# Seven products for eight transposed HGRN blocks, and token-major HGRN blocks in wide pairs

## Chip, cores, metric

One core of a Trainium2 chip runs the kernel. The metric is the device time of the run in microseconds (us); lower is better. The kernel before took 2633.77 us in the median of three runs (2633.15 to 2634.07).

## What is computed

One layer of an encoder on 1024 tokens of width 1024, in float32. Only the start of it matters here:

```python
z = rmsnorm(x, norm_mix_g[l])
proj = z @ w_in[l]                                   # 1024 x 1024 times 1024 x 11280
(ml_qk, ml_v, ml_o, ml_g, hg_q, hg_ff, hg_fb, hg_i, hg_g,
 gate_m, gate_h) = split_cols(proj, IN_SPLITS)
...
q_h = to_heads(jax.nn.silu(hg_q), HG_HEADS)          # per head a chunked scan, both directions,
v_h = to_heads(hg_i, HG_HEADS)                       # with forget gates from hg_ff and hg_fb
...                                                  # mLSTM, merge, W_out, cross attention,
x = x + (gelu(dwconv(up_a)) * up_b) @ w_down[l]      # and a gated FFN at the end
```

`hg_q`, `hg_ff` and `hg_fb` (3072 columns) are wanted transposed, channels by tokens. `hg_i` and `hg_g` (2048 columns) are wanted token-major.

## The kernel before, in words

Every engine has its own instruction stream, and they meet on semaphores. TensorE multiplies float32 in three passes of the fp32r type: each operand is split into a high part (a copy, `whi`, `a_hi`) and a low part (the rest, `wlo`, `a_lo`), and high x high, high x low and low x high are added up in PSUM.

Weights come in blocks (`Blk`). A block is 1024 rows x 256 columns, 1 MB, and goes to one of two slots of `raw`, by the parity of its number. For each block SP issues the load (`weights`, `stream`, L460) once the low part of the block two before is made; ACT makes the high part (`split_hi`, L853, a copy of 128x2048); DVE makes the low part (`split_lo`, L1383); PE multiplies; ACT copies the results out of PSUM to `ev` (`unit_out`, L864, four units of 512 columns a block) and issues their stores (`put_t`, `put_n`).

The stages around the change, in order:

- Nine blocks before it (memory keys and values, the mLSTM gates), till 85 us.
- `B_HGT`, 12 transposed blocks: `half_T` (L1979, matmul L1989) holds 128 weight columns stationary and moves 512 tokens. A block is 2 column tiles x 2 token halves x 8 contraction tiles x 3 passes = 96 matmuls of 512 columns. The first four blocks are written out, with the work on the mLSTM gate rows between them (DVE L1434 to L1463, ACT L955 to L960, PE's transposes of the gate rows at L2089 ahead of block 3); the other eight stand in a loop (L2092, ACT L971, DVE L1464). Results go to `hg_T` in DRAM.
- `B_HGN`, 8 token-major blocks: `half_N` (L2009, matmul L2020) holds 128 tokens stationary and moves the block's 256 weight columns, 8 token tiles x 8 x 3 = 192 matmuls of 256 columns. Results go to `hg_N`.
- `hg_pe` (L2099), 8 heads of the HGRN scan. Between its own small matmuls PE fills in the products of the mLSTM blocks (`dense`) in a fixed order. ACT's copy `level_keys` (L1016, L1026) and DVE's products feed it.

POOL meanwhile prepares the FFN's down projection, which is done much later: for each of 11 row blocks of `w_down` it loads 1 MB to `wd`, makes four sums of quarters (`quarter_sums`, L606, L611) in `wd_sums` and stores them, 1 MB, each step waiting for the one before (L616 to L621). Then it issues the loads of the first head's queries and gates (`load_q`, `qfb`, L629) when `hg_T` is complete, and of its values (`load_v`, L634) when `hg_N` is. The places of `wd` and `wd_sums` in SBUF are those of scan buffers.

The FFN's up projection (`win_pe`, L2414, matmul L2432) already uses the scheme of seven products: a block's product with all tokens is cut into 2 x 2 quarters (contraction halves, column or token halves), and seven products of sums of quarters replace eight. For a block of weights POOL makes four differences (`weight_sums`, L809, L817), ACT seven high parts (`factor_hi`, L1281) and one copy out of PSUM (L1328), DVE seven low parts (`factor_lo`, L1830) and seven additions out of PSUM (`product_out`, L1841). The sums of the input (four, of 128x2048) are made once (`operand_sum`, L1817, L1820; high parts L1268, low parts L1825). PE does 7 products x 4 contraction tiles x 3 passes = 84 matmuls of 512 columns. The down projection (`down_pe`, L2450) is made of seven products too, with tokens stationary and 512 columns moving.

## Time and profile before

| | |
|---|---|
| median of 3 runs | 2633.77 us |
| the profiled execution: its own time, its span | 2634.17 us, 2632.6 us |
| granted TensorE clock, mean | 0.995 |
| busy: PE matmul, DVE, ACT, POOL | 2591.4, 1462.5, 905.6, 607.0 us |
| busy share: DVE, ACT, POOL | 56%, 34%, 23% |
| DMA over the span | 348.96 MB, 133 GB/s |

The span runs from the first to the last instruction. PE is TensorE's matmuls, PEld its loads of the stationary side, which overlap them; DVE is VectorE, ACT ScalarE, POOL GpSimd, SP the engine that only issues DMAs. A matmul's duration includes its way through the array, so consecutive ones overlap: what one costs is the distance between starts. In a row, `out<-in xcount` tells the tiles written and read and the number of instructions; `L2020` is a line of the kernel.

### The profile page before, as it was taken

To read this page: it belongs to the slowest core of one execution; us is meant where nothing else is said; L and a number is where in the kernel's file an instruction comes from. 1 tells how busy PE (TensorE), PEld (TensorE's weight loads), DVE (VectorE), ACT (ScalarE), POOL (GpSimd) and SP (SyncE) were. 2 spreads that over 40 slices of the span, in tenths; PEclk is the share of its full clock that TensorE was granted. 3 is DMA by queue.
4 is the path that set the end of the run, shared out by engine and by line. 5 is a ranking of instruction groups with operands and counts; after the bars stand their busy time and mean duration, and the time that the engine had idled before them with its cause. 6 is when DMAs were issued, how large, how long until landed. Compare 5 with 4: busy or idle time off the path is not lost. (4 is left out here: it accounts for less than half of the span.)

```text
span 2632.6 us, 37140 instructions
## 1 busy us (share of the span) xinstructions
PE 2591.4 (98%) x14848; PEld 2277.7 (87%) x14848; DVE 1462.5 (56%) x1689; ACT 905.6 (34%) x1077; POOL 607.0 (23%) x553
## 2 busy tenths in 40 slices
PE   7999999999999999999999999999999999999998
PEld 7888899999999999988888788987798888888886
DVE  5511111277888888644443524343437998887566
ACT  6321211233343444322232523143314433343433
POOL 2014420011121222323331101000002565563001
PEclk9999999999999999999999999999999999999999
DMA  8345552223323333333431736101213232335754
GB/s 278 122 140 213 215 187 96 96 96 105 103 97 112 112 112 104 123 130 124 166 137 54 274 120 229 52 32 48 105 49 129 79 128 96 112 113 174 281 192 168
DMA packets 191426, 348.96 MB, mean 133 GB/s; under 512 B 9579, under 2 KB 125623, under 8 KB 191312
## 3 DMA queue, kind: packets, MB, share of 16 engines
q1 hardware_dynamic: 125152, 154.44, 17.7%
q0 software_dynamic: 32192, 118.44, 12.9%
q10 hardware_dynamic: 33968, 74.52, 7.4%
q8 instruction: 76, 1.25, 0.2%
q14 instruction: 38, 0.31, 0.0%
HBM read 241.10 MB, written 106.27 MB: 132 GB/s over the span
## 5 line engine op out<-in xcount | busy, mean ns | idle before, releaser
L2020 PE MATMUL ps<-whi,a_hi 128*128 128x256 f32 x1536 | 440.5, 287 | 0.8 <-DVE a_lo L1728 0.8
L2020 PE MATMUL ps<-whi,a_lo 128*128 128x256 f32 x1536 | 435.0, 283 | 0.0
L2020 PE MATMUL ps<-wlo,a_hi 128*128 128x256 f32 x1536 | 435.0, 283 | 0.0
L1386 DVE TENSOR_TENSOR wlo<-raw,whi 128x2048 fp32r<-128x2048 f32 x77 | 178.1, 2313 | 427.7 <-ACT whi L862 427.6
L1989 PE MATMUL ps<-a_hi,whi 128*128 128x512 f32 x864 | 347.7, 402 | 0.2 <-DVE a_lo L1405 0.2
L1989 PE MATMUL ps<-a_hi,wlo 128*128 128x512 f32 x864 | 336.9, 390 | 0.0
L1989 PE MATMUL ps<-a_lo,whi 128*128 128x512 f32 x864 | 336.5, 390 | 0.0
L867 ACT ACTIVATE ev<-ps 128x512 f32<-128x512 f32 x208 | 124.5, 598 | 508.2 <-PE ps L1989 290.2
L2020 PEld LDWEIGHTS ps<-whi,a_hi 128*128 128x128 f32 x1536 | 295.2, 192 | 1.6 <-DVE a_lo L1728 1.0
L2020 PEld LDWEIGHTS ps<-wlo,a_hi 128*128 128x128 f32 x1536 | 295.3, 192 | 0.4 <-issue 0.2
L2020 PEld LDWEIGHTS ps<-whi,a_lo 128*128 128x128 f32 x1536 | 295.0, 192 | 0.0
L862 ACT ACTIVATE whi<-raw 128x2048 fp32r<-128x2048 f32 x77 | 147.5, 1916 | 142.9 <-PE ps L2020 111.2
L1989 PEld LDWEIGHTS ps<-a_hi,wlo 128*128 128x128 f32 x864 | 162.2, 188 | 34.9
L1989 PEld LDWEIGHTS ps<-a_hi,whi 128*128 128x128 f32 x864 | 162.5, 188 | 31.7 <-DVE a_lo L1405 0.6
L1989 PEld LDWEIGHTS ps<-a_lo,whi 128*128 128x128 f32 x864 | 162.6, 188 | 31.2
L2130 PEld LDWEIGHTS ps<-X,Yc 128*128 128x128 f32 x896 | 114.6, 192 | 6.8 <-issue 2.4
L2130 PE MATMUL ps<-X,Yc 128*128 128x128 f32 x896 | 117.8, 285 | 0.2 <-DVE X L1547 0.2
L667 POOL TENSOR_TENSOR cv<-cv,cs 128x1024 f32<-128x1024 f32 x16 | 38.4, 2403 | 332.4 <-ACT cs L1034 332.4
L817 POOL TENSOR_TENSOR wt<-raw 128x512 f32<-128x512 f32 x36 | 82.6, 2296 | 136.3 <-DVE wlo L1830 97.5
L2432 PE MATMUL ps<-a_hi,whi 128*128 128x512 f32 x288 | 112.0, 389 | 0.0
L2432 PE MATMUL ps<-a_lo,whi 128*128 128x512 f32 x288 | 112.0, 389 | 0.0
L2432 PE MATMUL ps<-a_hi,wlo 128*128 128x512 f32 x288 | 112.0, 389 | 0.0
(360 smaller groups left out, 5403.9 us busy)
## 6 DMA issues: line engine op xcount, KB each, us to landing
raw<-in_w_in SPq DMA_DIRECT2D x45, 1024.0 KB, 5.0
raw<-in_w_up SPq DMA_DIRECT2D x22, 1024.0 KB, 5.1
hg_T<-ev ACTq DMA_DIRECT2D x24, 512.0 KB, 2.7
qfb<-hg_T POOLq DMA_DIRECT2D x24, 512.0 KB, 4.9
wd<-in_w_down POOLq DMA_DIRECT2D x11, 1024.0 KB, 5.3
down_weight_sums<-wd_sums POOLq DMA_DIRECT2D x11, 1024.0 KB, 4.7
hidden_T<-ga ACTq DMA_DIRECT2D x11, 1024.0 KB, 4.1
hidden_sums<-s POOLq DMA_DIRECT2D x10, 1024.0 KB, 4.9
```

The lines of the kernel that those rows point to most:

```text
L667: line(pool.tensor_tensor(cv[:], cv[:], cs[:], ALU.mult))
L817: signal(pool, pool.tensor_tensor(wt[:, i], x_, y_, ALU.subtract), s_t, weight_sum(n, i + 1))
L862: signal(act, act.activation(whi[:, b.slot], w4[:, b.slot], ACT.Copy), w_hi, b.count())
L867: signal(act, act.activation(ev[:, u], ps[:, u], ACT.Copy), ev_done, b.unit(u))
L1386: signal(dve, dve.tensor_tensor(wlo[:, b.slot], w4[:, b.slot], whi[:, b.slot], ALU.subtract), w_lo, b.count())
L1989: ins = pe.matmul(ps[:, u], W[sw][:, b.slot, k, c * P:(c + 1) * P], op[mw][:, k, t * HALF:(t + 1) * HALF], start=k == 0 and q == 0, stop=k ...
L2020: ins = pe.matmul(ps[:, u, part * BC:(part + 1) * BC], op[sw][:, k, t * P:(t + 1) * P], W[mw][:, b.slot, k], start=k == 0 and q == 0, stop ...
L2130: ins = pe.matmul(pair((l + 1) % 2, c), chunk(Yc, c), view(X, c * P, *dims), start=True, stop=True)
L2432: ins = pe.matmul(ps[:, bank], ring(W[sw], q)[:, k], op[mw][:, k], start=k == 0 and p_ == 0, stop=k == 3 and p_ == 2)
```

## The change

- The first four transposed blocks stay. The other eight (`B_HS`) are done with seven products of 84 matmuls in all, written out block by block. POOL makes the weights' four differences (`hs_weight_sums`), ACT and DVE the high and low parts quarter by quarter (`hs_hi`, `hs_lo`), ACT copies product 0 out and DVE adds the others out of PSUM (`hs_out`). Each of the seven products has its place in the weight buffer (`ring`).
- Four sums of the input are made between the first four blocks: two on DVE behind the first block's gate work, two after PE's gate transposes have read the gate rows, whose memory they share. DVE makes their low parts, ACT their high parts.
- The 8 token-major blocks become 4 pairs: a block is half the contraction (4 tiles) of 512 columns. PE goes through the 8 token tiles with the first block, one PSUM bank each, and again with the second, 768 matmuls of 512 columns in all. ACT copies out 8 banks per pair.
- The down-weight sums go behind `load_q(0)`. The next load of `wd` is issued once the sums have read it, just ahead of the store of the sums; each round waits for the load and for the last store. `wd` and `wd_sums` are moved to other scan buffers' places, and the first `level_keys` of ACT, the first convolution of DVE and POOL's `load_v(0)` wait for the last store.
- Semaphores of the FFN stages are shared with the new stage, with offsets on their counts.

```diff
+    sb("ahead_of_wd", [P, 14 * T - 2 * NT], F32, c)
     wd = sb("wd", [P, 2, D], F32, c)
+    sb("ahead_of_sums", [P, 2 * T], F32, c)
     wd_sums = sb("wd_sums", [P, 4, HALF], F32, c)
+with ExitStack() as c:
...
-    stream(B_HGN, 8, HG_N_COL)
+    with sp.Fori(0, 4) as i:
+        c = sp.snap(i * (2 * BC) + HG_N_COL)
+        for j in range(2):
+            b = Blk(B_HGN + j, i, 2)
+            sp.wait_ge(w_lo, b.count(-2))
+            sp.dma_start(wide(raw, b), w_in[:, 4 * j:4 * j + 4, at(c, 2 * BC)]).then_inc(w_ld[b.slot], 16)
...
-    for g in range(NFF):
-        pool.dma_start(wd[:], A["w_down"][0][g * BC:(g + 1) * BC, :].rearrange("(k p) n -> p k n", p=P)).then_inc(sum_io, 16)
-        pool.wait_ge(sum_io, 32 * g + 16)
+    def hs_weight_sums(n):
+        b = Blk(B_HS + n)
+        pool.wait_ge(w_ld[b.slot], b.slot_dmas())
+        if n:
+            pool.wait_ge(w_lo, b.count(-1))
+        b11, b12, b21, b22 = [w_quarter(b, k, c) for k in range(2) for c in range(2)]
+        for i, (x_, y_) in enumerate(((b12, b11), (b22, hwt[:, 0]), (b22, b12), (b21, hwt[:, 1]))):
+            signal(pool, pool.tensor_tensor(hwt[:, i], x_, y_, ALU.subtract), s_t, 4 * n + i + 1)
+    for n in range(N_HS):
+        hs_weight_sums(n)
+    def down_weights(g):
+        rows_ = A["w_down"][0][g * BC:(g + 1) * BC, :].rearrange("(k p) n -> p k n", p=P)
+        pool.dma_start(wd[:], rows_).then_inc(x_ld[3], 16)
+    def down_weight_sums(g):
+        pool.wait_ge(x_ld[3], 16 * g + 16)
+        if g:
+            pool.wait_ge(sum_io, 16 * g)
         line(quarter_sums(wd[:, 0, 0:HALF], wd[:, 0, HALF:D], wd[:, 1, 0:HALF], wd[:, 1, HALF:D], wd_sums, False))
+        if g + 1 < NFF:
+            down_weights(g + 1)
         pool.dma_start(wsum_d[g].rearrange("i p n -> p i n"), wd_sums[:]).then_inc(sum_io, 16)
-        pool.wait_ge(sum_io, 32 * g + 32)
...
+    down_weights(0)
+    for g in range(NFF):
+        down_weight_sums(g)
+    pool.wait_ge(sum_io, 16 * NFF)
     pool.wait_ge(st[0], 16 * 21)
     pool.wait_ge(st[1], 16 * 20)
...
+        if b.step or b.base != B_HS - 1:
+            split_hi(b.ahead(1))
+        else:
+            hs_sum_hi(2)
+            for q in range(3):
+                hs_hi(0, q)
...
+    def pair_out(b, col, t, stored):
+        u, c = t % 4, t // 2 % 2
+        if t % 2 == 0:
+            act.wait_ge(st[c], stored[c])
+        act.wait_ge(unit_done, b.unit(t))
+        signal(act, act.activation(ev[:, u], ps[:, t], ACT.Copy), ev_done, b.unit(t))
+        if t % 2:
+            act.dma_start(hN[(t - 1) * P:(t + 1) * P, at(col, 2 * BC)].rearrange("(u p) n -> p u n", p=P),
+                          ev[:, u - 1:u + 1]).then_inc(st[c], 16)
+    def pair_act(i, step, stored):
+        b = Blk(B_HGN, i, step) if step else Blk(B_HGN + 2 * i)
+        col = act.snap(i * (2 * BC)) if step else i * 2 * BC
+        split_hi(b.ahead(1))
+        split_hi(b.ahead(2), unit_done, b.unit(0))
+        for t in range(NT):
+            pair_out(b, col, t, [v + 16 * (t // 4) for v in stored])
...
+    def hs_sum_hi(i):
+        act.wait_ge(s_sum, i + 1)
+        signal(act, act.activation(hs[i][1][:], hs[i][0][:], ACT.Copy), hi_gelu, i + 1)
+    def hs_hi(n, q):
+        b = Blk(B_HS + n)
+        if q == 0:
+            act.wait_ge(w_ld[b.slot], b.slot_dmas())
+        if n:
+            act.wait_ge(prod_done if q < PRODUCTS - 1 else unit_done, hs_product(n - 1, q))
+        else:
+            act.wait_ge(unit_done, Blk(B_HS - (2 if q < 3 else 1)).unit(3))
+        if q in T_WAIT:
+            act.wait_ge(s_t, 4 * n + T_WAIT[q])
+        ins = act.activation(ring(whi, q), hs_operand(n, q), ACT.Copy)
+        if q < PRODUCTS - 1:
+            signal(act, ins, part_hi, hs_part(n, q))
+        else:
+            signal(act, ins, w_hi, b.count())
+    def hs_act(n):
+        b, final = Blk(B_HS + n), n == N_HS - 1
+        act.wait_ge(prod_done, hs_product(n, 0))
+        if n:
+            act.wait_ge(s_ev, PRODUCTS * (n - 1) + 3)
+        act.activation(hm1[:], ps[:, win_bank(n, 0)], ACT.Copy).then_inc(ev_done, 4)
+        act.wait_ge(ev_done, b.unit(3))
+        if final:
+            split_hi(Blk(B_HGN), prod_done, hs_product(n, 2))
+        for q in range(PRODUCTS) if not final else ():
+            hs_hi(n + 1, q)
+        for c in (1, 0):
+            act.wait_ge(s_ev, PRODUCTS * n + 7 - c)
+            put_t(hT, (4 + n) * BC)(c)
...
+    for q in range(3, PRODUCTS):
+        hs_hi(0, q)
+    hs_sum_hi(3)
+    for n in range(N_HS):
+        hs_act(n)
     with act.Fori(0, 3) as i:
-        for j in range(2):
-            col = act.snap(i * (2 * BC) + j * BC)
-            raw_block(Blk(B_HGN + j, i, 2), put_n(hN, col), (i * 32 + 16 * (13 + j), i * 32 + 16 * (12 + j)))
+        pair_act(i, 2, [i * 32 + 16 * 13, i * 32 + 16 * 12])
...
+                if not step:
+                    act.wait_ge(sum_io, 16 * NFF)
...
+    def hs_sum_lo(i):
+        dve.wait_ge(hi_gelu, i + 1)
+        signal(dve, dve.tensor_tensor(hs[i][2][:], hs[i][0][:], hs[i][1][:], ALU.subtract), lo_conv, (1, 2, 3, 4)[i])
+    def hs_lo(n, q):
+        dve.wait_ge(part_hi if q < PRODUCTS - 1 else w_hi, hs_part(n, q) if q < PRODUCTS - 1 else Blk(B_HS + n).count())
+        ins = dve.tensor_tensor(ring(wlo, q), hs_operand(n, q), ring(whi, q), ALU.subtract)
+        if q < PRODUCTS - 1:
+            signal(dve, ins, part_lo, hs_part(n, q))
+        else:
+            signal(dve, ins, w_lo, Blk(B_HS + n).count())
+    def hs_out(n, *which):
+        for i in which:
+            q = Q_OUT[i]
+            if i == 0:
+                dve.wait_ge(ev_done, Blk(B_HS + n).unit(3))
+            if i == 2:
+                dve.wait_ge(st[0], 16 * (4 + n + 1))
+            if i == 4:
+                dve.wait_ge(st[1], 16 * (4 + n))
+            dve.wait_ge(prod_done if q < PRODUCTS - 1 else unit_done, hs_product(n, q))
+            dst, x_ = ((hu2[:], hm1[:]), (hu3[:], hu2[:]), (ev[:, 0], hm1[:]), (hu4[:], hu2[:]),
+                       (ev[:, 3], hu3[:]), (ev[:, 2], hu4[:]), (ev[:, 1], hu3[:]))[i]
+            signal(dve, dve.tensor_tensor(dst, x_, ps[:, win_bank(n, q)], ALU.add), s_ev, PRODUCTS * n + i + 1)
...
+        if k < 3:
+            split_lo(Blk(B_HGT + k + 1))
+        if k == 3:
+            dve.wait_ge(g_tr, 1)
+            dve.wait_ge(rows_st, 32)
+            operand_sum(2, hs3[0][:], [(hi_(0, 0), ALU.subtract, hi_(0, 1)), (ALU.add, lo_(0, 0)), (ALU.subtract, lo_(0, 1))])
+            operand_sum(3, hs4[0][:], [(hi_(1, 0), ALU.subtract, hs2[0][:]), (ALU.add, lo_(1, 0))])
+            for i in (1, 2):
+                hs_sum_lo(i)
+            for q in range(PRODUCTS):
+                hs_lo(0, q)
+            hs_sum_lo(3)
...
+    for n in range(N_HS):
+        final = n == N_HS - 1
+        for q in range(3) if not final else ():
+            hs_lo(n + 1, q)
+        hs_out(n, 0, 1, 2, 3, 4)
+        if final:
+            split_lo(Blk(B_HGN))
+            hs_out(n, 5, 6)
+        else:
+            hs_lo(n + 1, 3)
+            hs_lo(n + 1, 4)
+            hs_out(n, 5)
+            hs_lo(n + 1, 5)
+            hs_out(n, 6)
+            hs_lo(n + 1, 6)
...
+    def hs_pe(n):
+        b = Blk(B_HS + n)
+        for q in range(PRODUCTS):
+            if q < PRODUCTS - 1:
+                pe.wait_ge(part_lo, hs_part(n, q))
+            else:
+                pe.wait_ge(w_lo, b.count())
+            if n == 0 and q in (1, 2, 4, 5):
+                pe.wait_ge(lo_conv, {1: 2, 2: 3, 4: 1, 5: 4}[q])
+            p, bank = PRODUCTS * n + q, win_bank(n, q)
+            if p < 4:
+                pe.wait_ge(grow_act, 4)
+            elif p < 8:
+                pe.wait_ge(ev_done, Blk(B_HS - 1).unit(bank))
+            else:
+                n0, q0 = divmod(p - 8, PRODUCTS)
+                if q0 == 0:
+                    pe.wait_ge(ev_done, Blk(B_HS + n0).unit(3))
+                else:
+                    pe.wait_ge(s_ev, PRODUCTS * n0 + LAST_READ[q0])
+            kh, th = {0: (0, 0), 3: (1, 0), 6: (1, 1)}.get(q, (0, 0))
+            op = hs[{1: 1, 2: 2, 4: 0, 5: 3}[q]][1:] if q in (1, 2, 4, 5) else [quarter(t, kh, th) for t in opA]
+            for k in range(4):
+                for p_, (sw, mw) in enumerate(((0, 0), (0, 1), (1, 0))):
+                    ins = pe.matmul(ps[:, bank], ring(W[sw], q)[:, k], op[mw][:, k],
+                                    start=k == 0 and p_ == 0, stop=k == 3 and p_ == 2)
+            if q < PRODUCTS - 1:
+                ins.then_inc(prod_done, 1)
+            else:
+                ins.then_inc(unit_done, 4)
+    for n in range(N_HS):
+        hs_pe(n)
+    def pair_pe(i, step):
         for j in range(2):
-            whole(half_T, Blk(B_HGT + j, i, 2), opA)
-    with pe.Fori(0, 4) as i:
-        for j in range(2):
-            whole(half_N, Blk(B_HGN + j, i, 2), opA)
+            b = Blk(B_HGN + j, i, step)
+            pe.wait_ge(w_lo, b.count())
+            for t in range(NT):
+                if j == 0 and step:
+                    pe.wait_ge(ev_done, b.unit(t, 2))
+                elif j == 0:
+                    if t < 3:
+                        pe.wait_ge(s_ev, PRODUCTS * (N_HS - 1) + LAST_READ[3 + t])
+                    elif t == 3:
+                        pe.wait_ge(s_ev, PRODUCTS * N_HS)
+                for k in range(4):
+                    for q, (sw, mw) in enumerate(((0, 0), (0, 1), (1, 0))):
+                        ins = pe.matmul(ps[:, t], opA[sw][:, 4 * j + k, t * P:(t + 1) * P], wide(W[mw], b)[:, k],
+                                        start=j == 0 and k == 0 and q == 0, stop=j == 1 and k == 3 and q == 2)
+                if j:
+                    ins.then_inc(unit_done, 1)
+    pair_pe(0, 0)
+    with pe.Fori(1, 4) as i:
+        pair_pe(i, 2)
```

## Rows read from the trace of the kernel before

**Rows 1.** The page's first part: busy time, share of the span, instructions.
```profile
PE 2591.4 (98%) x14848; PEld 2277.7 (87%) x14848; DVE 1462.5 (56%) x1689; ACT 905.6 (34%) x1077; POOL 607.0 (23%) x553
```

**Rows 2.** Stretches: length, then PE, PEld, DVE, ACT, POOL busy, clock, DMA.
```profile
85.06:152.34 67.28, 67.28 (x316) 55.67 (x315) 27.57 (x24) 24.81 (x27) 3.15 (x6) 1.00 0.29 96
152.34:348.33 195.99, 195.99 (x865) 162.26 (x865) 21.12 (x9) 38.08 (x47) 73.11 (x61) 1.00 0.57 203
348.33:532.64 184.31, 184.31 (x1537) 184.31 (x1536) 30.85 (x27) 38.70 (x43) 9.52 (x8) 1.00 0.32 111
2068.30:2410.80 342.50, 342.50 (x1512) 283.69 (x1511) 305.86 (x315) 135.14 (x174) 194.27 (x113) 1.00 0.31 111
2411.00:2620.00 209.00, 209.00 (x923) 173.11 (x922) 134.30 (x127) 82.69 (x82) 14.95 (x15) 1.00 0.66 227
```

**Rows 3.** Timeline of PE at both ends of the token-major stage: start, duration, instruction.
```profile
348.33 0.28 PE L2020 MATMUL ps<-whi,a_hi 128*128 128x256 f32 x1
348.44 0.28 PE L2020 MATMUL ps<-wlo,a_hi 128*128 128x256 f32 x1
...
532.64 1.95 PE L2115 MATMUL ps<-qs,Sall 128*128 128x128 f32 x16
...
537.16 2.82 PE L2130 MATMUL ps<-X,Yc 128*128 128x128 f32 x16
```

**Rows 4.** Groups of instructions, 2068 to 2411 us: busy, mean ns, idle before.
```profile
L817 POOL TENSOR_TENSOR wt<-raw 128x512 f32<-128x512 f32 x34 | 76.5, 2251 | 132.3 <-DVE wlo L1830 97.5 <-DMA hidden_sums<-s 33.5
L1830 DVE TENSOR_TENSOR wlo<-wt,whi 128x512 fp32r<-128x512 f32 x72 | 70.7, 982 | 8.3 <-ACT whi L1281 6.5
L1841 DVE TENSOR_TENSOR ev<-u,ps 128x512 f32<-128x512 f32 x53 | 36.4, 687 | 4.7 <-PE ps L2432 2.9
L1281 ACT ACTIVATE whi<-wt 128x512 fp32r<-128x512 f32 x70 | 44.3, 633 | 114.7 <-PE ps L2432 58.9 <-POOL wt L817 55.3
```

**Rows 5.** Single lines over the whole span: duration min/median/max in ns.
```profile
L817 POOL TENSOR_TENSOR wt<-raw x36: 1280/2152/3309, 2043.4 to 2379.8; 128x512 f32<-128x512 f32 x36
L1830 DVE TENSOR_TENSOR wlo<-raw,whi x54: 691/693/1704, 2066.7 to 2391.0; 128x512 fp32r<-128x512 f32 x54
```

**Rows 6.** Waits, 2068 to 2411 us: total us, times, longest.
```profile
POOL wt L817 <- DVE wlo L1830: 97.5, 9, 18.3
```

**Rows 7.** Timeline: PE at the gate transposes; DVE at the FFN's input sums.
```profile
152.00 0.41 PE L2090 MATMUL ps<-gds,ones 36*128 36x64 f32 x2
...
2033.92 3.28 DVE L1817 TENSOR_TENSOR s<-a_hi 128x2048 f32<-128x2048 f32 x1
...
2042.86 2.29 DVE L1817 TENSOR_TENSOR s<-a_hi,s 128x2048 f32<-128x2048 f32 x1
```

**Rows 8.** The page's costliest groups: ACT's copies.
```profile
L867 ACT ACTIVATE ev<-ps 128x512 f32<-128x512 f32 x208 | 124.5, 598 | 508.2 <-PE ps L1989 290.2
...
L862 ACT ACTIVATE whi<-raw 128x2048 fp32r<-128x2048 f32 x77 | 147.5, 1916 | 142.9 <-PE ps L2020 111.2
```

**Rows 9.** DMA issues, 170 to 370 us: size, median us to landing.
```profile
hg_T<-ev ACTq DMA_DIRECT2D x17, 512.0 KB, 2.9
```

**Rows 10.** Timeline of ACT at the start of head 0.
```profile
534.02 1.53 ACT L1026 ACTIVATE Yc<-Y 128x1024 f32<-128x1024 f32 x1 [0.53 <-ACT ev L867]
```

**Rows 11.** Timeline of POOL: first round of the down-weight sums, start of the last.
```profile
176.68 0.74 POOL L617 DMA_DIRECT2D wd<-in_w_down  x1 [38.77 <-ACTq L970]
182.01 1.29 POOL L611 TENSOR_TENSOR wd_sums<-wd 128x512 f32<-128x512 f32 x1 [4.59 <-DMA wd<-in_w_down]
...
187.71 0.82 POOL L620 DMA_DIRECT2D down_weight_sums<-wd_sums  x1 [0.30 <-POOL wd_sums L611]
...
346.58 0.71 POOL L617 DMA_DIRECT2D wd<-in_w_down  x1 [4.14 <-DMA down_weight_sums<-wd_sums]
```

**Rows 12.** Landing times of the loads of wd, then of the stores of wd_sums.
```profile
DMA to landing us min/median/max: 5.2/5.3/6.0
DMA to landing us min/median/max: 4.7/4.7/5.8
```

More of the change, by code:

```diff
@@ L64 @@
 B_HGN = B_HGT + 12
+B_HS = B_HGT + 4
+N_HS = B_HGN - B_HS
 B_ML = B_HGN + 8
@@ L83, with hs_part, hs_product @@
 N_DOWN = PRODUCTS * NFF
+PART0 = (PRODUCTS - 1) * N_HS
+TAKEN0 = PRODUCTS * N_HS
+Q_OUT = (1, 2, 3, 4, 4, 5, 6)
+LAST_READ = (0, 1, 2, 3, 5, 6, 7)
+def hs_part(n, q):
+    return (PRODUCTS - 1) * n + q + 1
+def hs_product(n, q):
+    return hs_part(n, q) if q < PRODUCTS - 1 else Blk(B_HS + n).unit(3)
 def weight_sum(n, i=4):
-    return 1 + 4 * n + n // 2 + i
+    return 4 * N_HS + 1 + 4 * n + n // 2 + i
 def hidden_sum(g):
     n = 2 * (g + 1 - PLAIN)
-    return 1 if g == 0 else 1 + 4 * min(n + 2, N_WIN) + n // 2 + 1
+    return 4 * N_HS + (1 if g == 0 else 1 + 4 * min(n + 2, N_WIN) + n // 2 + 1)
 def factor(n, q):
@@ L286, in build, with hs_sum @@
         with ExitStack() as c:
+            sb("ahead_of_wd", [P, 14 * T - 2 * NT], F32, c)
             wd = sb("wd", [P, 2, D], F32, c)
+            sb("ahead_of_sums", [P, 2 * T], F32, c)
             wd_sums = sb("wd_sums", [P, 4, HALF], F32, c)
+        with ExitStack() as c:
+            def hs_sum(name):
+                hi = sb(name + "_hi", [P, 4, HALF], F32R, c)
+                with ExitStack() as c1:
+                    f32 = sb(name, [P, 4, HALF], F32, c1)
+                return f32, hi, sb(name + "_lo", [P, 4, HALF], F32R, c)
+            hs1, hs2 = hs_sum("hs1"), hs_sum("hs2")
+            hm1 = sb("hm1", [P, HALF], F32, c)
+            hu2 = sb("hu2", [P, HALF], F32, c)
+            hs3, hs4 = hs_sum("hs3"), hs_sum("hs4")
+            hu3 = sb("hu3", [P, HALF], F32, c)
+            hu4 = sb("hu4", [P, HALF], F32, c)
+            hwt = sb("hwt", [P, 4, 4, P], F32, c)
+            hs = (hs1, hs2, hs3, hs4)
         with ExitStack() as c:
@@ L409, in build, with wide @@
         gt_ld, br_st = (gt_ld0, gt_ld1), (br_st0, br_st1)
+        def wide(t, b):
+            return t[:, b.slot].rearrange("p (k n) -> p k n", k=4) if len(t.shape) == 3 else t[:, b.slot].rearrange("p k n -> p (k n)").rearrange("p (k n) -> p k n", k=4)
         def quarter(t, kh, th):
@@ L926, in raw_block @@
             def raw_block(b, dst, stores):
-                split_hi(b.ahead(1))
+                if b.step or b.base != B_HS - 1:
[4 more added lines that the diff above has]
+                        hs_hi(0, q)
                 for c in range(2):
@@ L1085, in _ @@
             next_queries(0)
-            for j in (6, 7):
-                raw_block(Blk(B_HGN + j), put_n(hN, j * BC), (16 * (13 + j), 16 * (12 + j)))
+            pair_act(3, 0, [16 * 19, 16 * 18])
             hg_act(0, 0)
@@ L1427, in _, with operand_sum @@
             signal(dve, dve.tensor_tensor(lb_raw[:, :, 1], lb_raw[:, :, 0], lb_raw[:, :, 1], ALU.subtract), col_done, 1)
-            for k in range(4):
-                split_lo(Blk(B_HGT + k + 1))
+            def operand_sum(n, dst, terms):
+                (a, op, b_), rest = terms[0], terms[1:]
+                ins = dve.tensor_tensor(dst, a, b_, op)
+                for op, b_ in rest:
+                    line(ins)
+                    ins = dve.tensor_tensor(dst, dst, b_, op)
+                signal(dve, ins, s_sum, n + 1)
@@ L1463, in _ @@
                            grow_dve, 3)
-            with dve.Fori(2, 6) as i:
-                for j in range(2):
-                    split_lo(Blk(B_HGT + j + 1, i, 2))
+            for n in range(N_HS):
[13 more added lines that the diff above has]
+                    hs_lo(n + 1, 6)
             with dve.Fori(0, 3) as i:
@@ L2091, in _ @@
                 whole(half_T, Blk(B_HGT + k), opA)
-            with pe.Fori(2, 6) as i:
-                for j in range(2):
-                    whole(half_T, Blk(B_HGT + j, i, 2), opA)
-            with pe.Fori(0, 4) as i:
-                for j in range(2):
-                    whole(half_N, Blk(B_HGN + j, i, 2), opA)
+            def hs_pe(n):
+                b = Blk(B_HS + n)
+                for q in range(PRODUCTS):
[24 more added lines that the diff above has]
+                        ins.then_inc(prod_done, 1)
+                    else:
+                        ins.then_inc(unit_done, 4)
```

108 lines of the change are left out of this document (56 added, 52 removed).

## The prediction

> **What bounds the kernel now.** I read the page's busy times first: TensorE (PE) is busy 98% of the span [rows 1]. Then the table of stretches: from 85.06 to 532.64 us, the whole of the two HGRN projections, PE is busy in every microsecond at a granted clock of 1.00 [rows 2], and asked who PE waited for in that stretch the trace names nobody. So here the time is the number of matmuls times their spacing, as long as the other engines keep up. The busy time of one instruction (0.39 or 0.28 us) is not its price, since matmuls overlap; starts are. In the token-major stage they stand 0.12 us apart [rows 3]: 184.31 us for 1536 matmuls of 256 columns [rows 2] is 0.1200 us each. The 512-column stage has 9 blocks of 96 = 864 matmuls from 152.34 to 348.33: 0.2268. The seven-product stage of the FFN needs 342.50 us for 18 x 84 = 1512: 0.2265 [rows 2]. I use 0.2267 for 512 columns. Two 256-column matmuls cost 0.240 for the same columns, so a matmul pays about 0.013 us beside its columns.
>
> **Seven products.** Eight transposed blocks go from 96 matmuls to 84 each (7 products x 4 contraction tiles x 3 hi/lo passes), the columns of each being 512 as before. Removed: 8 x 12 x 0.2267 = 21.8 us, all of it on the path, since PE is the only engine without idle time there. A block then lasts 84 x 0.2267 = 19.04 us instead of 21.76.
>
> **Wide pairs.** Four pairs of token-major blocks take 4 x 192 = 768 matmuls of 512 columns in place of 1536 of 256: 184.3 - 768 x 0.2267 = 184.3 - 174.1 = 10.2 us. That such a matmul, with tokens as the stationary side and 512 weight columns moving, runs at the same spacing is seen in the down projection, which is of this form: 209.0 us for 923 [rows 2], 0.2264 each.
>
> The Trainium skill speaks against this second part. Its page "TensorE: Matmul & The Clock Gate", section "Back-to-back issue gap", gives a spacing of N / 2.4 + 2.5 ns when warm: 109.2 ns at 256 columns and 215.8 at 512. By that only 4 x 192 x 2.6 ns = 2.0 us could be saved by widening, and 96 x 0.2158 = 20.7 by the products, 22.7 in all, an estimate from that page. The trace does not agree: 120.0 and 226.7 ns at the full clock.
>
> **Work that joins PE's, and whether it keeps up.** For a seven-product block POOL makes 4 differences of weights, ACT 7 high parts and 1 copy, DVE 7 low parts and 7 additions out of PSUM. The chain that repeats from block to block: the low part of product 6 of block n frees the sum buffer; POOL's sums 1 to 3 for block n+1; ACT's high part of product 2; on DVE the low part of product 2, five additions, low parts 3 and 4, addition, low part, addition, low part of product 6. That is 3 sums, 1 high part, 5 low parts and 7 additions. With the mean durations of the FFN stage [rows 4]: 3 x 2.25 + 0.63 + 5 x 0.98 + 7 x 0.69 = 17.1 us. Low end, each sum at the shortest 1.28 and each low part at 0.69 [rows 5]: 12.8. High end, sums at the longest 3.31 and low parts at 1.70 [rows 5]: 23.9. PE's block gives it 19.04. I take "it keeps up, cost 0", because the nearest rows are the same chain: in the FFN stage DVE carries the convolution and the gating as well (305.86 us busy in 342.50 [rows 2], 89%; here 14 short operations a block, 7 x (0.98 + 0.69) = 11.7 of 19.04), POOL also the hidden sums, and PE stood still in none of 18 blocks; POOL itself waited 97.5 us there for the low parts [rows 6], which is slack.
>
> **Start of that stage.** Four sums of the input are needed first. Two (5 passes) fit into DVE's idle time behind the first block. The others (3 + 2 passes) wait for PE's gate transposes, since they lie on the gate rows' memory: released at 152.4 [rows 7], then 5 passes and 2 low parts of 2048 elements and one of 512 before product 0. A pass takes 2.29 us, or 3.28 beside POOL [rows 7]: 7 x 2.29 + 0.69 = 16.7 us ends at 169.1; 7 x 3.28 + 1.7 = 24.7 ends at 177.1. PE finishes the fourth block at 152.34 + 21.8 = 174.1. So 0 to 3 us; POOL's four sums last only some 8 us of it, so I take 0. ACT gets behind this wait (it holds the high parts ahead of evicting block 3), but these evictions are first needed by product 4, 11 us into the stage.
>
> **End of each stage.** Wide block 0 needs its whole half of the weight buffer, free after product 2 of the last block; the split, ACT 1.9 [rows 8] and DVE 2.3 us, fits into the four products left (10.9 us), though DVE first adds out product 4. In the pairs a PSUM bank is evicted every 2.72 us in 0.60 of ACT [rows 8]. Cost 0, bounded above by one split of 4 us if ACT were late. SP's loads stay 1 MB per block, well ahead; the wide ones come in 2 KB pieces.
>
> **What is moved.** The 11 down-weight sums (1 MB in, 4 POOL operations, 1 MB out) leave their place from 176.7 us on [rows 11], where POOL will make the new sums, and come behind the first head's query load. With seven products ending at 174.1 + 152.3 = 326.4 and the last store of hg_T landing about 4 us later (0.7 addition, 0.4 issue, 2.9 landing [rows 9]), POOL is through load_q(0) at 332 and has the first weights at about 338. Everything queued behind them on POOL, load_v(0) and load_q(1), and ACT's first level_keys wait for them. The pairs end at 326.4 + 174.1 = 500.5; by the distance in the old trace (532.64 to 534.02 for ACT's copy, 537.16 for PE's first use of it [rows 3, 10]) the sums must be stored by about 502 to 503.5. That leaves 164 us for 11 rounds, 14.9 a round. Before, a round took (346.58 - 176.68) / 10 = 17.0 us [rows 11], with load, sums and store one after another. Now the next load is issued just ahead of the store. If they overlap fully: sums 5.5 + 0.3 + load issue 0.7 + store 4.7 [rows 11, 12] = 11.2 a round, done at 461. If they only queue: 5.5 + 0.3 + 5.3 + 4.7 = 15.8, done at 512. I take 12.5 to 13.5, since transfers of 1 MB beside others in that stretch needed 6.0 and 5.8 us at the most against 5.3 and 4.7 [rows 12], and the new stretch has less traffic (DMA share 0.32 against 0.57 [rows 2]): done near 480, hidden with 20 us to spare.
>
> **Sum.** 21.8 + 10.2 = 32.0 us, nothing back. The profiled execution took 2634.17 us for a span of 2632.6, and becomes 2602.2; the median of the runs, 2633.77, is 0.4 below it, and becomes 2601.8. All that follows starts 32 us earlier and does not depend on a clock. No more than 32 can be won: PE has no idle time in the stage to give.
>
> **Rivals.**
> A. The down-weight sums end late. For: load and store are on one queue of POOL, and one buffer each. Against: the landings above. At 15.8 us a round they end at 512, and head 0 of the HGRN stage starts 8 to 10 us late: 2611. At the old 17.0 a round: 338 + 187 = 525, 22 us late: 2624. It decides from 14.9 us on.
> B. The operand chain paces the products. Between 19.04 and 23.04 us a block it eats the gain: at 21 us, 8 x 2 = 16 back, 2618. The other side: above 19.04 + 32.0 / 8 = 23.04 us a block the kernel is slower than before. At the high end of 23.9 the stage loses 8 x 4.86 = 38.9, so 6.9 us over before, 2641. It would take POOL losing every arbitration to DVE; the FFN stage, with more of both, has sums of 2.25 in the mean, not 3.31.
> C. The wide matmul brings no relief in this place, for instance because loading the stationary side bounds it and not the columns: 2 x 0.120 each, gain 21.8 only, 2612. Against: the down projection. The page's spacing named above would put the time at 2611.
> D. A stall at the seams (start of the products, first wide block) of 3 to 6 us: 2605 to 2608.
>
> **Chances.** Forecast, 2600.5 to 2604.5: 0.70. D 0.08. A 0.09. B below 23.04 us 0.06, above it 0.03. C 0.03. Rest 0.01. What can be told from no change is 0.2%, 5.3 us, so the bounds are 2628.5 and 2639.0. Faster takes all but the worst of B: 0.95; same 0.02; slower 0.03. The range runs from 2600 (spacings exactly as counted, a little less at the seams) to 2612, which takes in D, the milder half of A, and C; above it about 0.12 is left out.
>
> **What would show it.** Each seven-product block 19.04 us on PE, 84 starts 0.227 apart, no wait of PE for DVE's low parts; the first product within 1 us of 174; wide matmuls with starts 0.227 apart, 2.72 us a group of 12; the last one ending near 500.6 and PE's first HGRN scores starting 32 us earlier than 532.64. POOL's rounds between 11.2 and 14.9 us and its last store landed before 502. It is wrong if PE shows idle time in front of product matmuls (B, D) or in front of the first level's matmuls of head 0 (A), or if a wide matmul stands 0.24 from the next (C), or if a later stage, which the change does not touch, gives some of the 32 us back.

## The result, and the profile after

The changed kernel takes 2615.76 us in the median of four runs (2614.11 to 2616.20), the kernel before 2633.92 in four: a ratio of 0.993, 95% interval 0.9916 to 0.9943. It is faster by 18 us where the prediction had 32, and 2615.8 lies above the range of 2600 to 2612. The profiled execution took 2616.02 us for a span of 2614.5.

The page's first part, to be held against [rows 1]: busy time, share of the span and instructions of each engine.

```profile
PE 2559.2 (98%) x13984; PEld 2219.0 (85%) x13984; DVE 1569.7 (60%) x1807; ACT 918.8 (35%) x1105; POOL 653.0 (25%) x585
```

PE issues 14848 - 13984 = 864 matmuls fewer, as counted: 96 in the products, 768 in the pairs. TensorE's busy time fell by 32.2 us, the span by only 18.1, so about 14 us of standing still are new.

The stretches of the two stages, and of the two that follow them: start and end, length, then PE, PEld, DVE, ACT and POOL busy, granted clock, DMA share, GB/s.

```profile
175.00:326.96 151.96, 151.96 (x672) 125.84 (x671) 88.20 (x111) 42.66 (x64) 41.01 (x28) 1.00 0.32 108
326.96:501.00 174.04, 174.04 (x769) 144.17 (x768) 33.94 (x28) 38.17 (x42) 69.96 (x64) 1.00 0.70 231
502.00:520.00 18.00, 5.51 (x29) 4.70 (x29) 1.23 (x1) 3.38 (x2) 9.02 (x10) 0.70 0.48 184
520.00:560.00 40.00, 40.00 (x255) 36.37 (x254) 32.87 (x26) 14.99 (x16) 3.18 (x3) 0.96 0.28 96
```

Both stages are without idle time on PE at a clock of 1.00. The stretch behind them has PE at work for 5.5 of 18 us. The timeline of PE names the place (start, duration, instruction, idle time before it and its releaser):

```profile
174.41 0.39 PE L2184 MATMUL ps<-a_hi,wlo 128*128 128x512 f32 x1
174.64 0.39 PE L2312 MATMUL ps<-a_hi,whi 128*128 128x512 f32 x1
...
326.73 0.39 PE L2312 MATMUL ps<-a_hi,wlo 128*128 128x512 f32 x1
326.96 0.39 PE L2336 MATMUL ps<-whi,a_hi 128*128 128x512 f32 x1
...
500.81 0.39 PE L2336 MATMUL ps<-whi,a_lo 128*128 128x512 f32 x1
501.04 1.16 PE L2363 MATMUL ps<-qs,Sall 128*128 128x128 f32 x9
...
518.23 3.75 PE L2380 MATMUL ps<-X,Yc 128*128 128x128 f32 x16 [12.49 <-ACT Yc L1165]
```

The first product starts at 174.64, the pairs at 326.96 (152.32 / 8 = 19.04 us a block), the first scores of head 0 at 501.04, which is 31.6 us ahead of [rows 3]. Up to here the prediction (32 us ahead) holds to half a microsecond. Then PE waits 12.5 us for ACT's copy Yc, and the waits from 85 to 620 us (total, times, longest) say for what ACT waited:

```profile
PE ps L2380 <- ACT Yc L1165: 12.5, 1, 12.5
ACT Yc L1165 <- DMA down_weight_sums<-wd_sums: 14.7, 1, 14.7
POOL wd_sums L659 <- DMA down_weight_sums<-wd_sums: 88.7, 10, 12.3
POOL wd_sums L659 <- DMA wd<-in_w_down: 7.1, 1, 7.1
```

It is the last store of the down-weight sums, the place of rival A. POOL's own rounds, first and last, with the copy that is released:

```profile
336.82 0.72 POOL L680 DMA_DIRECT2D wd<-in_w_down  x1
344.61 1.28 POOL L659 TENSOR_TENSOR wd_sums<-wd 128x512 f32<-128x512 f32 x1 [7.06 <-DMA wd<-in_w_down]
...
350.26 0.74 POOL L680 DMA_DIRECT2D wd<-in_w_down  x1 [0.30 <-POOL wd_sums L659]
351.00 0.78 POOL L690 DMA_DIRECT2D down_weight_sums<-wd_sums  x1
361.00 1.29 POOL L659 TENSOR_TENSOR wd_sums<-wd 128x512 f32<-128x512 f32 x1 [9.22 <-DMA down_weight_sums<-wd_sums]
...
511.89 0.77 POOL L690 DMA_DIRECT2D down_weight_sums<-wd_sums  x1 [0.30 <-POOL wd_sums L659]
516.58 1.50 ACT L1165 ACTIVATE Yc<-Y 128x1024 f32<-128x1024 f32 x1 [14.69 <-DMA down_weight_sums<-wd_sums]
```

The last sums start at 506.32, so a round takes (506.32 - 344.61) / 10 = 16.2 us. It is the store that ends each round: POOL waited for it in all ten, 88.7 us, and for a load only in the first. The landing times of the loads, then of the stores, against [rows 12]:

```profile
DMA to landing us min/median/max: 6.8/6.9/7.7
DMA to landing us min/median/max: 4.6/9.3/12.9
```

The load took 1.6 us longer than before, the store, issued 0.74 us behind it, twice as long. The shortest store, 4.6, is the last one, which had no load beside it.

### The profile page after: what moved, and what is told of

The parts are those of the page before. It is cut to its first block and busy times, and to the rows that moved or that the text cites. A ratio compares the mean times of both kernels' runs of the same rounds, so it can differ in the third digit from the quotient of the medians.

```text
span 2614.5 us, 35682 instructions
## 1 busy us (share of the span) xinstructions
PE 2559.2 (98%) x13984; PEld 2219.0 (85%) x13984; DVE 1569.7 (60%) x1807; ACT 918.8 (35%) x1105; POOL 653.0 (25%) x585
## 3 DMA queue, kind: packets, MB, share of 16 engines
q1 hardware_dynamic: 121056, 154.44, 17.7%
## 5 line engine op out<-in xcount | busy, mean ns | idle before, releaser
L2215 PE MATMUL ps<-whi,a_hi 128*128 128x256 f32 x1024 | 295.7, 289 | 0.2 <-DVE a_lo L1935 0.2
L2215 PE MATMUL ps<-wlo,a_hi 128*128 128x256 f32 x1024 | 290.4, 284 | 0.0
L2215 PE MATMUL ps<-whi,a_lo 128*128 128x256 f32 x1024 | 290.3, 284 | 0.0
L2184 PE MATMUL ps<-a_hi,whi 128*128 128x512 f32 x608 | 248.6, 409 | 0.2 <-DVE a_lo L1543 0.2
L2184 PE MATMUL ps<-a_hi,wlo 128*128 128x512 f32 x608 | 237.6, 391 | 0.0
L2184 PE MATMUL ps<-a_lo,whi 128*128 128x512 f32 x608 | 237.4, 390 | 0.0
L2215 PEld LDWEIGHTS ps<-whi,a_hi 128*128 128x128 f32 x1024 | 196.8, 192 | 0.9 <-DVE a_lo L1935 0.4
L2215 PEld LDWEIGHTS ps<-wlo,a_hi 128*128 128x128 f32 x1024 | 197.0, 192 | 0.3 <-issue 0.2
L2215 PEld LDWEIGHTS ps<-whi,a_lo 128*128 128x128 f32 x1024 | 196.8, 192 | 0.0
L2184 PEld LDWEIGHTS ps<-a_hi,wlo 128*128 128x128 f32 x608 | 114.3, 188 | 24.9
L2184 PEld LDWEIGHTS ps<-a_hi,whi 128*128 128x128 f32 x608 | 114.8, 189 | 21.8 <-DVE a_lo L1543 0.6
L2380 PE MATMUL ps<-X,Yc 128*128 128x128 f32 x896 | 118.8, 287 | 12.7 <-ACT Yc L1165 12.5
L2682 PE MATMUL ps<-a_hi,wlo 128*128 128x512 f32 x288 | 112.1, 389 | 0.0
L2682 PE MATMUL ps<-a_lo,whi 128*128 128x512 f32 x288 | 112.1, 389 | 0.0
L2682 PE MATMUL ps<-a_hi,whi 128*128 128x512 f32 x288 | 112.1, 389 | 0.0
```

Of the source, the lines that this page charges most:

```text
L2184: ins = pe.matmul(ps[:, u], W[sw][:, b.slot, k, c * P:(c + 1) * P], op[mw][:, k, t * HALF:(t + 1) * HALF], start=k == 0 and q == 0, stop=k ...
L2215: ins = pe.matmul(ps[:, u, part * BC:(part + 1) * BC], op[sw][:, k, t * P:(t + 1) * P], W[mw][:, b.slot, k], start=k == 0 and q == 0, stop ...
L2380: ins = pe.matmul(pair((l + 1) % 2, c), chunk(Yc, c), view(X, c * P, *dims), start=True, stop=True)
L2682: ins = pe.matmul(ps[:, bank], ring(W[sw], q)[:, k], op[mw][:, k], start=k == 0 and p_ == 0, stop=k == 3 and p_ == 2)
```

## The experiments

In what follows a round is always (issue of the last store - issue of the first) / 10; measured so, the changed kernel's is (511.89 - 351.00) / 10 = 16.1 us. And "the wait" is PE's in front of Yc in head 0. The kernels of E1, E2, E3 and E8 ran on one chip (before: 2633.64 us, seven runs), E4 to E7 on another (before: 2635.77, nine runs), E9 alone (before: 2635.27, thirteen runs).

**E1: two buffers for the sums.** Stores alternate between two buffers and two semaphores, so that a round no longer needs the store just issued.

```
+            wd_sums2 = sb("wd_sums2", [P, 4, HALF], F32, c)
...
-                if g:
-                    pool.wait_ge(sum_io, 16 * g)
-                line(quarter_sums(wd[:, 0, 0:HALF], ..., wd_sums, False))
+                if g >= 2:
+                    pool.wait_ge(stored, 16 * (g // 2))
+                line(quarter_sums(wd[:, 0, 0:HALF], ..., dst, False))
                 if g + 1 < NFF:
                     down_weights(g + 1)
-                pool.dma_start(wsum_d[g]..., wd_sums[:]).then_inc(sum_io, 16)
+                pool.dma_start(wsum_d[g]..., dst[:]).then_inc(stored, 16)
```

> The changed kernel with a second buffer for the down-weight sums (8 KB, in the place of vg, which is loaded only afterwards), so that the sums of a round wait for the store two rounds back; the load of the next weights is still issued once the sums have read them. Output complete. Theory (the down-weight rounds end too late, because each waits 7.9 to 12.3 us for a store that lies behind the next load): a round now waits for the load alone, 5.7 us of sums and issue + 6.9 us to landing = 12.6 to 13.5 us, 344.6 + 10 x 13 + 5.7 + 5 = 485 us at the end, before the 502 at which the first level of head 0 wants it. PE's wait of 12.5 us and the low clock behind it (0.70 and 0.96, about 1.4 us) go: 2602.0 us (2601 to 2604). Rival 1 (the two stages' DMA traffic sets the pace, 2 MB a round beside weights and hg_N, whatever waits for what): rounds stay at 15 to 16.3 us, 2612 to 2616. Rival 2 (what is missing was lost elsewhere, the wait only hides it): PE's wait goes, but the time stays above 2608.

Measured: 2601.55 us (2599.69 to 2603.37), ratio 0.9873 [0.9856, 0.9889]. POOL's wait in the same stretch:

```profile
POOL wd_sums L662 <- DMA wd<-in_w_down: 66.8, 11, 8.4
```

The landings, loads first:

```profile
DMA to landing us min/median/max: 6.6/7.1/9.8
DMA to landing us min/median/max: 4.7/9.7/12.7
```

The stores are as slow as in the changed kernel, but nobody waits for them; PE's wait is gone altogether, and the time is 0.5 from the 2602.0 expected for this kernel, and 0.3 from the 2601.8 that the prediction forecast for the change. The round, now load, sums and issues, is (494.40 - 350.72) / 10 = 14.4 us, longer than the 12.6 to 13.5 expected. The last store is issued at 494.40, 17.5 us earlier. That the wait costs more than itself is read from the first and the last scores of the stage's heads, 501.04 and 1016.38 us in the changed kernel:

```profile
500.50 1.95 PE L2370 MATMUL ps<-qs,Sall 128*128 128x128 f32 x16
...
1001.57 1.95 PE L2370 MATMUL ps<-qs,Sall 128*128 128x128 f32 x16
```

515.3 against 501.1 us is 14.3 for a wait of 12.5. The granted clock fits the rest. The changed kernel in slices of 10 us from 510 (columns as above):

```profile
510.00:520.00 10.00, 1.77 (x8) 1.80 (x9) 1.23 (x1) 3.38 (x2) 5.50 (x8) 0.50 0.39 144
520.00:530.00 10.00, 10.00 (x53) 8.92 (x52) 8.66 (x7) 3.93 (x5) 0.18 (x1) 0.85 0.97 329
530.00:540.00 10.00, 10.00 (x66) 9.00 (x66) 8.27 (x8) 2.72 (x3) 0.00 (x0) 1.00 0.01 2
```

While PE stands still the granted clock falls to 0.50, 1.2 GHz, and it stands at 0.85 in the mean of the slice behind it; in E1 these three slices stand at 1.00. In slices of 2 us it is 0.50 from 510 to 522, 0.76 in the next and 1.00 from 524. An estimate from these: between 518.2 and 524 PE lost up to 2.4 us of work at the full clock, and the 1.8 us that are to be explained lie within that. No run takes the clock apart from the wait.

**E2: two buffers for the loads, store issued first.**

```
-                pool.dma_start(wd[:], rows_).then_inc(x_ld[3], 16)
+                pool.dma_start((wd, wd2)[g % 2][:], rows_).then_inc(x_ld[3 - g % 2], 16)
...
-                if g + 1 < NFF:
-                    down_weights(g + 1)
                 pool.dma_start(wsum_d[g]..., wd_sums[:]).then_inc(sum_io, 16)
+                if g + 2 < NFF:
+                    down_weights(g + 2)
```

> The changed kernel with a second buffer for the loaded down weights (in the place of vg), the first two loads issued at once, later ones two rounds ahead and behind the store of the sums; one buffer for the sums. Output complete. Theory: the store is the first of its pair in POOL's queue and lands in 4.7 to 7 us, the load has a whole round to land; a round is 5.7 + 0.8 + 4.7 to 7 = 11.2 to 13.5 us, last store landed by 344.6 + 1 + 10 x 12.4 + 11 = 481; time 2602.0 us (2601 to 2604), the same as with two sum buffers. Rival 1 (DMA traffic sets the pace): rounds of 15 to 16.3 us, 2612 to 2616. Rival 2 (lost elsewhere): above 2608 without PE's wait.

Measured: 2603.70 us (2601.34 to 2605.64), ratio 0.9883 [0.9867, 0.99], no wait. The landings, loads first:

```profile
DMA to landing us min/median/max: 7.0/8.3/10.2
DMA to landing us min/median/max: 4.6/5.4/7.0
```

A round is (471.08 - 349.47) / 10 = 12.2 us, about the size that the prediction had forecast (12.5 to 13.5). The store lands in 5.4 when it is issued ahead of the load; now the load is the late one, and a second buffer covers it.

**E3: the order alone.** One buffer each, as in the changed kernel.

```
                 line(quarter_sums(...))
+                pool.dma_start(wsum_d[g]..., wd_sums[:]).then_inc(sum_io, 16)
                 if g + 1 < NFF:
                     down_weights(g + 1)
-                pool.dma_start(wsum_d[g]..., wd_sums[:]).then_inc(sum_io, 16)
```

> The changed kernel with one thing turned round: in each down-weight round the store of the sums is issued ahead of the next load. One buffer each, as before. Output complete. Theory (one after the other in time, and both needed before the next sums, so the order is without effect): the load now lands last, 9 to 10 us after its issue, rounds stay at 15.5 to 16.3 us and the time at 2616 (2614 to 2618). Rival (the order costs: a store behind a load is held up, a load behind a store is not, since reads and writes overlap that way round): rounds of 12 to 14 us and 2602 to 2605.

Measured: 2606.24 us (2605.11 to 2608.32), ratio 0.9892 [0.9875, 0.9908]; PE's wait, and the landings, loads first:

```profile
PE ps L2380 <- ACT Yc L1165: 1.8, 1, 1.8
```

```profile
DMA to landing us min/median/max: 7.0/8.3/9.7
DMA to landing us min/median/max: 4.7/5.4/6.4
```

The time lies between what was expected (2614 to 2618) and the rival (2602 to 2605). I had the order down as worth nothing, and it is worth 1.1 us a round, ten times: (499.83 - 349.91) / 10 = 15.0 us. What comes second is late in either order, but a load behind a store (0.8 + 8.3 = 9.1 us from the first issue) less than a store behind a load (0.7 + 9.3 = 10.0).

**E8: the load issued by SyncE**, so that the pair is not on one queue (SP waits for POOL's sums of the round, then issues the load between its own weight loads).

```
+                rows_ = A["w_down"][0][g * BC:(g + 1) * BC, :].rearrange(...)
+                sp.dma_start(wd[:], rows_).then_inc(kv_st0, 16)
...
+            for g in range(NFF):
+                down_weights(g)
+                if g in (2, 3, 5, 6):
+                    pair_load({2: 4, 3: 5, 5: 6, 6: 7}[g])
```

> The changed kernel with the loads of the down weights issued by SP on its queue, in a fixed order between its weight loads (each when POOL has made the sums of the round before); the stores stay with POOL. One buffer each. Output complete. It tells whether the queue or the DMA engines make the store late. Theory 1 (one queue of POOL: the store's descriptors stand behind the load's): on two queues both land in about 6 us, rounds of 5.7 + 0.8 + 6 = 12.5 to 13 us, no wait of PE, 2602 to 2604. Theory 2 (the 16 engines need that long for 2 MB beside the other traffic, on whatever queue): rounds stay at 15 to 16.3, PE waits 3 to 13 us, 2606 to 2616.

Measured: 2617.86 us (2617.32 to 2619.58), ratio 0.9934 [0.9917, 0.9951], a wait of 13.0 us, rounds of (511.50 - 348.56) / 10 = 16.3. A round's issues, and the landings of loads and stores:

```profile
362.89 0.37 SPq L553 DMA_DIRECT2D wd<-in_w_down  x1
363.16 0.78 POOL L702 DMA_DIRECT2D down_weight_sums<-wd_sums  x1 [0.30 <-POOL wd_sums L678]
```

```profile
DMA to landing us min/median/max: 6.0/6.3/9.4
DMA to landing us min/median/max: 4.6/9.8/11.3
```

Two queues, issues 0.3 us apart, and the store is as late as before. POOL's queue is not what puts the pair in a row. That was theory 2, though the time lies 1.9 us above its 2606 to 2616.

**E4: the changed kernel again**, on the second chip.

> The changed kernel once more, unaltered, as the mate of the next three on one chip: 2616 us (2614 to 2618), PE's wait for the first level 12.5 us. No theory differs on it.

Measured: 2615.06 us (2613.96 to 2615.96), ratio 0.9922 [0.9906, 0.9939], the wait again 12.5 us. The result is not that of one chip. The stores landed after 8.9 us in the median here, against 9.3 for the same kernel, so differences of a few tenths between such medians mean little.

**E5: the wide pairs alone** in the kernel before (transposed blocks with 96 matmuls, down-weight sums in their old place).

```
+            pair_pe(0, 0)
+            with pe.Fori(1, 4) as i:
+                pair_pe(i, 2)
-            with pe.Fori(0, 4) as i:
-                for j in range(2):
-                    whole(half_N, Blk(B_HGN + j, i, 2), opA)
```

> The kernel before with the wide pairs alone: 12 plain transposed blocks, the down-weight sums where they were (done at 365 us, long before the pairs end). Output complete. Theory (the matmul count holds, what is missing is only the late sums): 1536 x 0.1200 - 768 x 0.2267 = 10.2 us less, 2623.5 us (2622 to 2625), no wait of PE in the stage. Rival (widening brings less than counted, because of its seams, evictions or loads): 2625 to 2632.

Measured: 2626.21 us (2620.39 to 2628.22, six runs), ratio 0.9967 [0.9955, 0.998]; no wait of PE. The first scores start at 521.95 instead of 532.64, 10.7 us earlier, of which 10.2 are the pairs. The median of the runs missed the theory's 2622 to 2625 by 1.2 us and lies in the rival's range. Against its own chip's kernel before it shows 9.6; the interval of the ratio, 5.3 to 11.9 us, holds the term, and it is the trace that shows it.

**E6: the products alone**, token-major blocks of 256 columns, sums moved as in the changed kernel.

```
-            pair_pe(0, 0)
-            with pe.Fori(1, 4) as i:
-                pair_pe(i, 2)
+            for u in range(4):
+                ...
+                half_N(Blk(B_HGN), u, 0, opA)
+                half_N(Blk(B_HGN), u, 1, opA)
+            whole(half_N, Blk(B_HGN + 1), opA)
+            with pe.Fori(1, 4) as i:
+                for j in range(2):
+                    whole(half_N, Blk(B_HGN + j, i, 2), opA)
```

> The changed kernel with the token-major blocks as they were before, 256 columns wide; seven products and late down-weight sums as in the change. Output complete. Theory (one deadline for both parts): the token-major stage ends 10.2 us later, at 511 us, the sums at 512 to 516.5 as in the change, so PE waits 0 to 2.5 us instead of 12.5, and the time is 2612 to 2615, the same as or below the whole change's 2616: as it stands the widening has bought nothing. Rival (the two parts add up, the wait belongs to the seven products or to the head's start and not to a deadline): PE still waits 12 us and the time is 10 us above the change's, 2626.

Measured: 2621.91 us (2621.39 to 2623.88), ratio 0.995 [0.9934, 0.9967], a wait of 8.7 us: neither expectation. POOL's first sums, and those that were long:

```profile
346.45 1.29 POOL L654 TENSOR_TENSOR wd_sums<-wd 128x512 f32<-128x512 f32 x1 [9.01 <-DMA wd<-in_w_down]
...
400.18 3.22 POOL L654 TENSOR_TENSOR wd_sums<-wd,wd_sums 128x512 f32<-128x512 f32 x1
446.35 2.61 POOL L654 TENSOR_TENSOR wd_sums<-wd 128x512 f32<-128x512 f32 x1 [7.95 <-DMA down_weight_sums<-wd_sums]
478.49 2.83 POOL L654 TENSOR_TENSOR wd_sums<-wd 128x512 f32<-128x512 f32 x1 [7.38 <-DMA down_weight_sums<-wd_sums]
495.55 3.19 POOL L654 TENSOR_TENSOR wd_sums<-wd 128x512 f32<-128x512 f32 x1 [8.32 <-DMA down_weight_sums<-wd_sums]
```

I had carried the sums' end over from the changed kernel and moved only the scores by 10.2 us. But the sums ended later here too, last store at 518.24 instead of 511.89: the first load came 2 us later, and four sums took 2.6 to 3.2 us (1.3 us else) where the changed kernel has one of 2.1 and one of 1.6. Each of the four ran beside an operation of DVE with two operands. So with one sum buffer the widening is worth 2621.9 - 2615.1 = 6.8 us, not 10.2.

**E7: E6 with the two sum buffers of E1.**

```
+                stored, dst = (sum_io, x_ld[2])[g % 2], (wd_sums, wd_sums2)[g % 2]
```

> As the run before it (seven products, token-major blocks 256 wide), and with two buffers for the down-weight sums. Output complete. Theory: no wait of PE, the seven products' 96 matmuls x 0.2267 = 21.8 us in full, 2612 us (2610 to 2613.5); against it the kernel with both parts and two buffers (2601.55) shows the widening's 10.2. Rival (part of what was won since lies in the buffers' DMA pattern, not in the wait): below 2610 or above 2614.

Measured: 2611.83 us (2611.56 to 2613.33), ratio 0.9912 [0.9896, 0.9929], no wait. Against its chip's 2635.77 that is 23.9 for the products (21.8 counted), and E1, by its ratio, is 9.5 us below it (10.2 counted). With the sums out of the way both parts bring what was counted, within about 2 us.

**E9: no overlap at all.** Store first, and the next load only when it has landed.

```
+                pool.dma_start(wsum_d[g]..., wd_sums[:]).then_inc(sum_io, 16)
                 if g + 1 < NFF:
+                    pool.wait_ge(sum_io, 16 * g + 16)
                     down_weights(g + 1)
-                pool.dma_start(wsum_d[g]..., wd_sums[:]).then_inc(sum_io, 16)
```

> One edit to the changed kernel: the store of the down-weight sums is issued first and the next load only when that store has landed, so the 1 MB transfers never overlap. My theory (a load and a store of 1 MB in flight together take about as long as one after the other, so the overlap written into the changed kernel buys only about 1 us a round): every transfer lands in its time alone again, load about 5.3 and store about 4.7 us, the round is the old 17.0 us instead of 16.2, the sums end 8 us later than in the changed kernel, TensorE waits 12.5 + 8 = 20.5 us instead of 12.5 for ACT's copy in head 0, and the time is about 2623 to 2625. The rival (overlap pays for itself, and what makes the transfers slow is the stage's other traffic, the wide weight loads above all): load and store stay near 6.9 and 9.3 us also when each is alone, the round is 0.7 + 6.9 + 5.5 + 0.3 + 0.8 + 9.3, about 23 us, TensorE waits some 80 us, and the time is about 2685.

Measured: 2633.87 us (2630.29 to 2639.01, ten runs), ratio 0.9998 [0.9988, 1.0008]: the whole gain is gone. PE's wait, the landings of loads and stores, and the stretches of the pairs and of the standstill:

```profile
PE ps L2381 <- ACT Yc L1166: 28.9, 1, 28.9
```

```profile
DMA to landing us min/median/max: 5.2/5.4/8.5
DMA to landing us min/median/max: 4.6/4.6/6.0
```

```profile
326.96:500.00 173.04, 173.04 (x766) 143.30 (x765) 34.50 (x27) 38.16 (x42) 70.24 (x58) 1.00 0.62 223
502.00:532.00 30.00, 2.57 (x12) 1.76 (x10) 0.00 (x0) 0.22 (x1) 12.38 (x12) 0.58 0.40 151
```

The theory is confirmed in what it is about: in the same stage, beside the same weight loads, each transfer alone lands in 5.4 and 4.6 us, so the rival (the stage's traffic) falls. Its time was too low by 9: the round is (527.07 - 349.98) / 10 = 17.7 us, not 17.0, because three loads still took more than 8 us and some sums 3.2. Overlapping the pair therefore buys 17.7 - 16.1 = 1.6 us a round.

**What a wait costs.** All kernels do the same work on PE from the first to the last of the scores in eight heads. The kernel before, then E9:

```profile
L2115 PE MATMUL ps<-qs,Sall x128: 270/275/275, 532.6 to 1035.4; 128*128 128x128 f32 x128
L2364 PE MATMUL ps<-qs,Sall x128: 270/275/275, 499.9 to 1032.8; 128*128 128x128 f32 x128
```

That is 502.8 us before and 532.9 in E9. The kernels with the change and without a wait, E1, E2 and E7, need 502.4 to 502.8. With waits of 1.8 (E3), 8.7 (E6), 12.5 (the changed kernel; E4), 13.0 (E8) and 28.9 us (E9) it is 505.0, 512.9, 517.1 (516.4), 516.6 and 532.9. Against the 502.8 before, a wait costs itself and 0.4 to 1.8 us more, and the longest did not add more than a short one. The medians of the runs don't show this as finely: E9 is 32.3 us above E1, but in the traces 2.1 of the difference lie behind the heads, and E2 is 2.2 above E1 with no wait in either.

## Why the prediction was wrong

**The step that failed** is in the part on what is moved: "I take 12.5 to 13.5, since transfers of 1 MB beside others in that stretch needed 6.0 and 5.8 us at the most against 5.3 and 4.7 [rows 12] ... done near 480, hidden with 20 us to spare." A round took 16.2 us, and the last store landed at 516.5. In [rows 12] each transfer had its partner's time to itself, since load, sums and store came one after another; those rows could not show what a load and a store cost together. Together they need 0.7 + 9.3 = 10.0 us, which is what they need one after the other (5.4 + 4.6 in E9). The second reason given, "less traffic (DMA share 0.32 against 0.57 [rows 2])", compared unlike things: the 0.57 holds the down-weight transfers themselves, the 0.32 hardly any of them, and with them moved in the share is 0.70. E9, with the stage's other traffic as it was, shows that this misreading is not what made the transfers late. The prediction's own bound for that case, 5.5 + 0.3 + 5.3 + 4.7 = 15.8 us and "done at 512", came to within 5 us of the truth, and I had put rival A at 9%. Part of that is luck: 512 counts eleven whole rounds from 338, but the last round has no load behind it. By the same terms the end is 338 + 10 x 15.8 + 5.5 + 0.3 + 4.7 = 506.5, ten early: 6.6 for the first weights (below), the rest for rounds of 16.2. The bound from the other end, full overlap, had no row behind it at all. E1 shows the step to be the whole error: with the store off POOL's path the time is 2601.55, against a forecast of 2601.8.

**A second miss in the same step**: "has the first weights at about 338". They were there at 344.6, and this is 6.6 of the 12.5 us. By itself it would have cost nothing: the first sums started as late in E1 and E2 (344.3 and 343.8), which have no wait. The timeline where the products end, and the landing of these last two stores of hg_T:

```profile
325.71 0.37 SPq L544 DMA_DIRECT2D raw<-in_w_in  x1
...
326.33 1.95 ACTq L1017 DMA_DIRECT2D hg_T<-ev  x2
...
332.97 0.37 SPq L544 DMA_DIRECT2D raw<-in_w_in  x1
...
335.19 1.64 POOL L698 DMA_DIRECT2D qfb<-hg_T  x3 [38.73 <-DMA hg_T<-ev]
```

```profile
hg_T<-ev ACTq DMA_DIRECT2D x2, 512.0 KB, 6.9
```

The first of the two stores goes out 0.6 us behind 1 MB of weights that SP loads for the pairs, the second 1.6 us later at 327.95, and they land in 6.9 us instead of the 2.9 of [rows 9]. This is again a median used in a place where one engine's freed buffer starts another's load. That the load of wd took 7.8 us instead of 5.3 to its first sum has the same look: it is issued right behind the three loads of qfb and 3.9 us behind SP's next load. This part was read from the trace only; no run removes SP's loads there. Their width is not the reason: E6 has loads of 256 columns, and its first sums start later still, at 346.45.

**Rival A** had the mechanism and the place. Its sizes were "8 to 10 us late: 2611" at 15.8 a round (3 to 4.5 late, by the end at 506.5 above); it was 12.5 us at 16.2, and 1.8 more, which no term had, most likely for the clock that fell while PE stood still. 31.6 - 12.5 - 1.8 = 17.3 of 18.2 us. The last microsecond lies behind the heads: from the last scores to the end the changed kernel took 1596.4 us, the kernel before 1597.2, and the traces of the experiments range from 1593.7 (E5) to 1601.3 (E8).

**What was right.** The seven products, 21.8 us: blocks of 19.04 us, starts 0.227 apart. The wide pairs, 10.2 us: 174.08 us from 326.96 to 501.04, for a forecast of 174.1; the spacing of 226.7 ns, so that rival C falls. The 215.8 ns of the page "TensorE: Matmul & The Clock Gate" in the Trainium skill, section "Back-to-back issue gap", which the page calls the gap of an isolated matmul, and by which only 22.7 us could be had, did not hold for this stream either. The start of the products: 174.64 after a fourth block that began at 152.73, 0.15 us beyond what its matmuls need, so no stall (rival D). The operand chain (rival B): no wait of PE in 672 matmuls, and POOL stood idle for DVE's low parts for 87.6 us in eight blocks. The prediction also named the right marks for the move, "rounds between 11.2 and 14.9 us" and "its last store landed before 502": they failed, at 16.2 and 516.5, where the time did.

**A version that beats both.** E1: the change with a second sum buffer, 2601.55 us, 32 us below the kernel before and 14 below the changed one.
